# Where and how a two-layer transformer kernel makes its 24 modulation chunks, and the layout of one small projection

## The chip, the cores and the metric

The kernel runs on one core of a Trainium2 chip. The metric is device time in microseconds (us) of one execution. Its engines are TensorE (PE, with its weight loads PEld), VectorE (DVE), ScalarE (ACT), GpSimd (POOL) and SyncE (SP); matmul results go to PSUM, eight banks of 128 partitions by 512 float32. Everything is float32, and a profiled float32 matmul shows as two instructions (x2).

## The reference

Two layers over 256 context and 512 latent tokens of width 1024. What matters here:

```python
for layer in range(DEPTH):
    mod_l = split(silu(c)     @ ada_w[layer] + ada_b[layer], 6)     # 1024 x 6144 weights, 24 MB a layer
    mod_c = split(silu(c_ctx) @ ada_w[layer] + ada_b[layer], 6)
    p = modulate(rmsnorm(x, norm_mix_g), mod[0], mod[1]) @ w_in      # 1024 x 3104, 32 columns are kr
    y = concat(mla(p), swa(p), na(p), retention(p)) * mix_beta
    x = x + mod[2] * (y @ w_out)
    h2 = modulate(rmsnorm(x, norm_ffn_g), mod[3], mod[4])
    x = x + mod[5] * peer_ffn(h2)                                    # product-key experts, gathered rows
return rmsnorm(x_latent, final_norm_g)
```

`mla`, `swa` and `na` are softmax attentions with four heads each; `kr` is a 32-wide key part shared by the heads of `mla`. In the second layer only latent tokens are queries.

## The kernel before, in words

**Tokens.** 768 tokens are six tiles of 128. `hT` holds the normalised input turned, eight blocks of 128 features by 768 tokens; `yT` the mixers' output in the same form. Layer one works on six tiles, layer two on the four latent ones (keys of all six).

**Weights.** SP streams all large weights through `wring`, three slots of 1 MB, in one order fixed by `send`. A slot is sent again once PE signals that it has read it. One modulation chunk (512 of the 6144 columns) takes two slots; twelve chunks make one layer's modulation.

**A modulation chunk.** On PE L486 multiplies the two conditioning vectors by four row blocks of a slot in four 32-column strips of the array at once, for two slots: 16 instructions in the profile. ACT copies the bank out (L885), PE adds the four strips with L474 and the bias with L476 (two matmuls, four instructions), ACT copies the two rows out (L876) and stores them to HBM (L878). Chunks alternate between banks 6 and 7. The first four chunks of layer one's modulation (M=0) come first of all. The other eight stand between the six tiles of the first normalisation (`MOD_BETWEEN`): DVE normalises a tile (L1253, L1254), PE turns it (L510), ACT copies it to `hT` (L926). The twelve chunks of layer two's modulation (M=1) are made in layer one as well: 0 and 1 after the projection c5 and before the state matmuls L716; 2 to 4 behind L716; 5 and 6 between the two halves of the output projection; 7 to 11 between the tiles of the second normalisation (`MOD_BEFORE_FFN`).

**The kr projection.** After the first normalisation L523 makes `kr`: for each of six tiles eight matmuls with a 128x128 block of `hT` as weights and 32 moving columns, 48 in all. ACT copies it to `krrow` (L939). Then the projection chunks follow (L456 for those in token rows, L667 to L679 for those in feature rows).

**Attention.** Each of the three attentions goes over 24 items in layer one (six tiles by four heads; the first eight, of the context, have 256 keys, the others 768, 512 to 640, or 512) and 16 in layer two. PE in iteration i: `scores(i)` (L606, banks 0 to 3), `turn(i-2)`, which turns the probabilities (L618, banks 4 and 5), and for even i `values(i/2-2)` (L647), which makes the output of a pair of items, in bank 6 or 7 by the pair's parity. `scores(i)` waits for the exponential of item i-2, `turn(i)` for its normalisation. ACT in iteration i: exponential of item i (L1014), normalisation of item i-1 (L1021), and for even i from 6 on `y_out(i/2-3)`, which copies a pair's output to `yT` (L1003). DVE: the row maximum (L1325), a reciprocal, and the copy of the turned probabilities (L1344).

**Retention and the rest.** L716 makes six tiles of state updates; DVE chains them to states (L1384), and PE waits for the last (`st`) before the retention loop (L740, L751, L754, L730). Then the output projection (L456 with `yT`) in two chunks, with DVE's gated residual (L1431, L1433) under it, the second normalisation, the first queries of the expert FFN (L790), and the expert stage, which gathers 1280 rows of 8 KB for each of 128 partitions over both layers (L1673).

## Time and profile before

| | us |
|---|---|
| three runs | 4973.15, 4973.56, 4980.19 (median 4973.56) |
| the profiled execution: its own time | 4968.76 |
| its span in the trace | 4967.0 |
| first normalisation, from 59.85 to the start of kr at 116.51 | 56.7 |
| the three attentions of layer one: from 260.0, 337.4 and 508.0 | 77.4, 81.1, 74.7 |
| end of c5 to the retention loop, 667.66 to 707.46 | 39.8 |
| retention loop to the first queries of the FFN, 707.46 to 891.17 | 183.7 |
| expert stage of layer one, about 907 to 2957 | 2050 |

Of the span PE is busy 66%, DVE 63%, POOL 30%, ACT 18%. In the page's slices the 16 DMA engines are at 9 tenths in the expert stages (about 910 to 2950 and 3620 to the end) and at 0 to 3 tenths in the mixer stages, but for the first slice. The page is to be read by stage: in the mixer stages one engine follows another and nothing else is in flight, so that a stretch on PE there moves the end by its whole length; in the expert stages the gathers fix the pace. The times in the rows are us from the start of the span; idle time before a group stands in brackets with what ended it. A window row gives the stretch and its length, then the busy time with the number of instructions of PE, PEld, DVE, ACT and POOL, then the granted TensorE clock (as a share of 2.4 GHz; 1.00 or 0.50 at any one moment, so that a mean lies between), the DMA engines' busy share, and GB/s.

### The profile page before, as it was taken

The page shows a single profiled execution, that of the slowest core. Times are in us where ns is not written, and L with a number is a line of the kernel's source. Part 1 is how long each engine was busy: PE and PEld are TensorE (multiplying, and loading weights), DVE is VectorE, ACT ScalarE, POOL GpSimd, SP SyncE. Part 2 cuts the span into 40 slices and gives each one's busy share as a digit, 9 for nine tenths or more (in the row PEclk, how much of TensorE's full clock was granted, in tenths as well). Part 3 has the DMA queues.
Part 4 walks back from the last instruction along what each step waited for, and adds up shares of the span by engine and source line. Part 5 has one row for each costly group of instructions (what it writes and reads, how often), then busy time and mean ns, then how long its engine had stood idle before and what let it go on. Part 6 is the DMA issues. An engine that isn't in the chain of part 4 may idle for free.

```text
span 4967.0 us, 49025 instructions
## 1 busy us (share of the span) xinstructions
PE 3289.4 (66%) x16328; PEld 1296.2 (26%) x16328; DVE 3127.8 (63%) x8329; ACT 916.4 (18%) x2477; POOL 1492.6 (30%) x1376
## 2 busy tenths in 40 slices
PE   6989898665786555555555558898877455554554
PEld 1455553331232111111111115555422111111111
DVE  1052332587877878778877861513378787877876
ACT  2152321111111111111111121422111111111211
POOL 0000000233444443444444430000043444444443
PEclk8879889887898777777776768788888877777777
DMA  8100033899999999999999971011299999999998
GB/s 285 36 9 26 22 111 122 336 412 416 406 418 415 401 417 406 412 419 405 418 415 406 415 295 45 1 34 39 75 402 395 414 406 418 404 419 416 400 420 345
DMA packets 290751, 1496.73 MB, mean 301 GB/s; under 512 B 25433, under 2 KB 83929, under 8 KB 126657
## 3 DMA queue, kind: packets, MB, share of 16 engines
q0 software_dynamic: 185888, 1347.13, 65.9%
q1 hardware_dynamic: 73680, 114.85, 6.8%
q10 hardware_dynamic: 30928, 31.61, 1.9%
q8 instruction: 129, 2.11, 0.2%
q14 instruction: 126, 1.02, 0.1%
HBM read 1482.91 MB, written 10.58 MB: 301 GB/s over the span
## 4 chain that ended last, share of the span: by engine, by line
DVE 38%; PE 30%; DMA 19%; issue 7%; ACT 4%; POOL 1%; DVEq 1%; ACTq 0%; POOLq 0%; SPq 0%
DMA X<-in_uv_dram,X 17%; DVE X L1552 16%; PE ps L456 9%; PE ps L823 5%; PE ps L606 2%; DVE X L1563 2%; PE ps L647 2%; PE ps L790 2%; ACT X L1170 2%; PE ps L618 1%; POOL X L1673 1%; DVE X L1471 1%; DVE X L1469 1%; DVE X L1472 1%; DVE X L1559 1%
## 5 line engine op out<-in xcount | busy, mean ns | idle before, releaser
L823 PE MATMUL ps<-X 64*64 64x512 f32 x2560 | 1648.7, 778 | 1399.3 <-DVE X L1563 1384.7
L1673 POOL DMA_INDIRECT X<-in_uv_dram,X x1280 | 1417.2, 1107 | 2194.8 <-PE ps L826 1613.4
L1552 DVE CUSTOM_DVE_ANT_0 X<-yT,X 128x1024 f32<-128x1024 f32 x1280 | 1532.4, 1223 | 338.8 <-DMA X<-in_uv_dram,X 290.0
L826 PE MATMUL ps<-X 64*64 64x512 f32 x2560 | 1649.0, 778 | 0.0
L825 PE MATMUL ps<-X 64*64 64x512 f32 x2560 | 1649.0, 778 | 0.0
L824 PE MATMUL ps<-X 64*64 64x512 f32 x2560 | 1648.8, 778 | 0.0
L823 PEld LDWEIGHTS ps<-X 64*64 64x64 f32 x2560 | 360.5, 163 | 2621.0 <-DVE X L1563 1951.9
L1170 ACT ACTIVATE X<-X 128x1 f32<-128x1 f32 x1280 | 258.6, 203 | 2335.7 <-DVE X L1552 2268.9
L825 PEld LDWEIGHTS ps<-X 64*64 64x64 f32 x2560 | 360.7, 163 | 0.0
L826 PEld LDWEIGHTS ps<-X 64*64 64x64 f32 x2560 | 360.6, 163 | 0.0
L824 PEld LDWEIGHTS ps<-X 64*64 64x64 f32 x2560 | 360.5, 163 | 0.0
L790 PE MATMUL ps<-hT,wring 128*128 128x512 f32 (+1 forms) x768 | 314.0, 548 | 2.2 <-ACT hT L926 2.2
L456 PE MATMUL ps<-wring,hT 128*128 128x512 f32 (+2 forms) x736 | 304.8, 576 | 2.0 <-DVE X L1296 1.0
L1563 DVE TENSOR_TENSOR X<-wukv,X 128x128 f32<-128x128 f32 x640 | 187.2, 292 | 68.4 <-DVE X L1559 3.7
L1646 POOL TENSOR_TENSOR X<-X 128x256 f32<-128x256 f32 x32 | 23.0, 722 | 634.9 <-DVE att L1329 625.1
L1559 DVE TENSOR_TENSOR X<-X 128x2 f32<-128x2 f32 x640 | 102.9, 161 | 174.0 <-ACT X L1170 161.9
L606 PE MATMUL ps<-X 64*128 64x256 f32 (+3 forms) x464 | 182.4, 533 | 9.8 <-ACT X L1014 6.6
L1325 DVE TENSOR_REDUCE att<-ps 128x1 f32<-128x512 f32 (+3 forms) x120 | 87.0, 725 | 154.4 <-PE ps L606 152.2
L790 PEld LDWEIGHTS ps<-hT,wring 128*128 128x128 f32 x768 | 141.9, 198 | 161.9 <-issue 153.4
L456 PEld LDWEIGHTS ps<-wring,hT 128*128 128x128 f32 x736 | 138.6, 193 | 163.2 <-issue 159.1
L456 PE MATMUL ps<-wring,yT 128*128 128x512 f32 x320 | 146.6, 620 | 8.2 <-DVE X L1409 3.5
L618 PE MATMUL ps<-ident,X 128*128 128x128 f32 x512 | 103.7, 339 | 51.9 <-ACT X L1021 51.9
(232 smaller groups left out, 3481.5 us busy)
## 6 DMA issues: line engine op xcount, KB each, us to landing
wring<-in_ada_w_dram SPq DMA_DIRECT2D x48, 1024.0 KB
wring<-in_w_in_dram SPq DMA_DIRECT2D x24, 1024.0 KB
wring<-in_peer_wq_dram SPq DMA_DIRECT2D x24, 1024.0 KB
X<-in_uv_dram,X POOLq DMA_INDIRECT x1280
wring<-in_w_out_dram SPq DMA_DIRECT2D x8, 1024.0 KB
X<-scores ACTq DMA_DIRECT2D x64, 128.0 KB
X<-mods ACTq DMA_DIRECT2D x15, 512.0 KB, 6.7
yT<-mods ACTq DMA_DIRECT2D x8, 512.0 KB
```

What stands on the lines that cost most here:

```text
L456: m = pe.matmul(ps[:, t, c0:CH], hT_or_y[0][:, k, t * P:(t + 1) * P], wring[:, g % WRING, kk, c0:CH], start=(k == 0), stop=(k == KD - 1))
L606: m = pe.matmul(ps[:, 2 * (i % 2) + at // 512, at % 512:at % 512 + c], q, k[:, first + done:first + done + c], start=True, stop=True)
L618: m = pe.transpose(ps[:, 4 + b // 4, (b % 4) * P:(b % 4 + 1) * P], pr3[:, i % 3, b * P:(b + 1) * P], ident[:, :])
L790: m = pe.matmul(ps[:, 4 + j % 2, 0:N], by_columns(wq[0])[:, k, j % 2 * P:(j % 2 + 1) * P], hT[:, k, c0:c0 + N], start=(k == 0), stop=(k == ...
L823: pe.matmul(ps[0:HD, h, :], dg(slice(0, HD), s), v0[0:HD], **ends)
L824: pe.matmul(ps[HD:P, 2 + h, :], dg(slice(HD, P), s), v0[HD:P], **ends)
L825: pe.matmul(ps[HD:P, h, :], dg(slice(0, HD), s + 1), v1[0:HD], **ends)
L826: m = pe.matmul(ps[0:HD, 2 + h, :], dg(slice(HD, P), s + 1), v1[HD:P], **ends)
L1170: nc.scalar.activation(agel[:, s:s + 1], adot[:, s:s + 1], ACT.Gelu).then_inc(S("gel"), 1)
L1552: v.tensor_tensor_reduce(uvr[:, slot, 0:D], h2[:, t, :], uvr[:, slot, 0:D], 1.0, 0.0, ALU.mult, ALU.add, adot[:, s_:s_ + 1]).then_inc(S("d ...
L1563: v.tensor_tensor(dgs[:, s_ % DGRING:s_ % DGRING + BATCH, :], ident2.unsqueeze(1).to_broadcast([P, BATCH, HD]), adot[:, both].unsqueeze(2) ...
L1673: g.indirect_dma_start(uvr[:, slot, :], None, a["uv"], bass.IndirectOffsetOnAxis(ap=istages[i % 2][:, s:s + 1], axis=0)).then_inc(S(f"uv{s ...
```

## The change

Four parts.

1. `MOD_LATE` lists 20 chunks: 4 to 11 of M=0 and 0 to 11 of M=1. Six are made in each of the three attentions of layer one (at pairs 0, 2, 4, 6, 8, 10 of 12), the last two in the retention. `late_parts` (the L486 work) stands behind `values(p)`, `late_sum` (the L474 and L476 work) behind `values(p+1)`. The first normalisation, the output projection and the second normalisation have no chunk left in them. SP's order follows.
2. In all attentions of both layers `values` uses bank 7 for each pair and waits for the copy of the pair before it (formerly the one before that); the late chunks have bank 6. ACT's `y_out(p)` moves one iteration up, to i = 2p+5.
3. On ACT `late_rows` and `late_out` (the work of L885, L876, L878 and the bias load) stand behind `y_out`.
4. `kr` is made columnwise in both layers: `wkr` is the weights, 32 columns wide, and `hT` moves, in eight matmuls of 512 and eight of 256 tokens. ACT copies 32x768 out, six small transposes in the middle of the first projection chunk turn it to token rows, and ACT copies those to `krrow`.

```diff
-MOD_BEFORE_FFN = ((7, 8), (9,), (10,), (11,), (), ())
-MOD_EARLY = (2, 5, 7)
-MOD_BETWEEN = ((4, 5, 6), (7,), (8,), (9,), (10,), (11,))
+MOD_LATE = [(0, c) for c in range(MOD_FIRST, ADA_CHUNKS)] + [(1, c) for c in range(ADA_CHUNKS)]
+MOD_PAIRS = (0, 2, 4, 6, 8, 10)
+MOD_KINDS = {"mla": MOD_LATE[0:6], "swa": MOD_LATE[6:12], "na": MOD_LATE[12:18]}
+MOD_LAST = MOD_LATE[18:]
...
+        mod_late = (view(96 * K, [CH]), view(98 * K, [CH]))
...
-            for c in range(1, ADA_CHUNKS):
+            for c in range(1, MOD_FIRST):
                 send(0, a["ada_w"][0], c * CH, "mpp", c + 1, True)
...
-                    after = {len(stream) - 1: mod[:MOD_EARLY[1]], len(stream): mod[MOD_EARLY[1]:MOD_EARLY[2]], len(stream) + 1: mod[MOD_EARLY[2]:]}
+                    after = {1: mod[0:12], 3: mod[12:18], 5: mod[18:]}
...
+                def late_parts(M, c):
+                    pe.wait_ge(S("mrow"), B("mrow", M) + c)
+                    for half in range(2):
+                        g = take(1)
+                        for j in range(GROUP_K):
+                            m = pe.matmul(ps[32 * j:32 * j + 32, 6, :], cT[:, half * GROUP_K + j, :], wring[:, g % WRING, j, :],
+                                          start=(half == 0), stop=(half == 1))
+                        m.then_inc(S("mpp" if half else "w_half"), 1)
+                def late_sum(M, c):
+                    pe.wait_ge(S("mpc"), B("mpc", M) + c + 1)
+                    pe.matmul(ps[0:2, 6, :], pick, mod_late[0], start=True, stop=False)
+                    pe.wait_ge(S(f"ab{c % 2}"), B(f"ab{c % 2}", M) + 16 * (c // 2 + 1))
+                    pe.matmul(ps[0:2, 6, :], ones[0:1, 0:2], mod_late[1][0:1, :], start=False, stop=True).then_inc(S("mps"), 1)
...
-                for t in range(TILES):
-                    for k in range(KD):
-                        m = pe.matmul(ps[:, 7, t * 32:(t + 1) * 32], hT[:, k, t * P:(t + 1) * P], wkr[:, k, :],
-                                      start=(k == 0), stop=(k == KD - 1))
+                for k in range(KD):
+                    pe.matmul(ps[0:32, 6, :], wkr[:, k, :], hT[:, k, 0:CH], start=(k == 0), stop=(k == KD - 1))
+                for k in range(KD):
+                    m = pe.matmul(ps[0:32, 7, 0:TOK - CH], wkr[:, k, :], hT[:, k, CH:TOK], start=(k == 0), stop=(k == KD - 1))
                 m.then_inc(S("kr"), 1)
-                rows_chunk(L, range(TILES), S("c0"), ctx_from=384)
+                def turn_kr():
+                    pe.wait_ge(S("krx"), B("krx", L) + 1)
+                    for t in range(TILES):
+                        m = pe.transpose(ps[:, 7, TOK - CH + t * 32:TOK - CH + (t + 1) * 32], kr_cols[:, t * P:(t + 1) * P], ident[0:32, 0:32])
+                    m.then_inc(S("krp"), 1)
+                rows_chunk(L, range(TILES), S("c0"), turn_kr, ctx_from=384)
...
                     def values(p):
                         pe.wait_ge(S("a_pt"), ab + 2 * p + 2)
-                        if p >= 2:
-                            pe.wait_ge(S("a_ye"), ab // 2 + p - 1)
+                        if p >= 1:
+                            pe.wait_ge(S("a_ye"), ab // 2 + p)
...
+                        p = i // 2 - 2
                         if i >= 4 and i % 2 == 0:
-                            values(i // 2 - 2)
+                            values(p)
+                            if L < LAST and p in MOD_PAIRS:
+                                late_parts(*MOD_KINDS[kind][MOD_PAIRS.index(p)])
+                            if L < LAST and p - 1 in MOD_PAIRS:
+                                late_sum(*MOD_KINDS[kind][MOD_PAIRS.index(p - 1)])
                     pe.wait_ge(S("a_ye"), ab // 2 + N // 2)
+                    if L < LAST:
+                        M, c = MOD_KINDS[kind][-1]
+                        pe.wait_ge(S("mrow"), B("mrow", M) + c + 1)
...
-                    modulation(L + 1, range(0, MOD_EARLY[0]))
+                    late_parts(*MOD_LAST[0])
                 for t in range(TILES):
+                    if L < LAST and t == CT:
+                        late_sum(*MOD_LAST[0])
...
-                    modulation(L + 1, range(MOD_EARLY[0], MOD_EARLY[1]))
-                    pe.wait_ge(S("mrow"), B("mrow", L + 1) + MOD_EARLY[1])
+                    late_parts(*MOD_LAST[1])
+                    late_sum(*MOD_LAST[1])
+                    pe.wait_ge(S("mrow"), B("mrow", L + 1) + ADA_CHUNKS)
...
-                if L < LAST:
-                    modulation(L + 1, range(MOD_EARLY[1], MOD_EARLY[2]))
...
+                def late_rows(M, c):
+                    act.wait_ge(S("mpp"), B("mpp", M) + c + 1)
+                    if (M, c) != MOD_LATE[0]:
+                        M_, c_ = MOD_LATE[MOD_LATE.index((M, c)) - 1]
+                        act.wait_ge(S(f"ms{c_ % 2}"), B(f"ms{c_ % 2}", M_) + 16 * (c_ // 2 + 1))
+                    nc.scalar.activation(mod_late[0], ps[:, 6, :], ACT.Copy).then_inc(S("mpc"), 1)
+                def late_out(M, c):
+                    act.wait_ge(S("mps"), B("mps", M) + c + 1)
+                    if (M, c) != MOD_LATE[-1]:
+                        load_bias(*MOD_LATE[MOD_LATE.index((M, c)) + 1])
+                    nc.scalar.activation(mod_late[0][0:2, :], ps[0:2, 6, :], ACT.Copy).then_inc(S("mrow"), 1)
+                    act.wait_ge(S("mrow"), B("mrow", M) + c + 1)
+                    act.dma_start(mods[M, :, c * CH:(c + 1) * CH], mod_late[0][0:2, :]).then_inc(S(f"ms{c % 2}"), 16)
...
-                        if i >= 6 and i % 2 == 0:
-                            y_out(i // 2 - 3)
+                        p = (i - 5) // 2
+                        if i >= 5 and i % 2:
+                            y_out(p)
+                        if L < LAST and i >= 5 and i % 2 and p in MOD_PAIRS:
+                            late_rows(*MOD_KINDS[kind][MOD_PAIRS.index(p)])
+                        if L < LAST and i >= 7 and i % 2 and p - 1 in MOD_PAIRS:
+                            late_out(*MOD_KINDS[kind][MOD_PAIRS.index(p - 1)])
```

The lines of the changed kernel have other numbers: L488 and L501 are the L486 of before, L476/L478 and L507/L509 its L474/L476, L525 its L510, L627 its L606, L639 its L618, L668 its L647, L458 its L456, L1060 its L1014, L1067 its L1021, L1049 its L1003.

PE, the end of the first normalisation of layer one, kr and the first projection chunk, before:

```order
L486 MATMUL ps<-wring,cT 32x512 x8
L474 MATMUL ps<-X,ones 2x512
L476 MATMUL ps<-X,ones 2x512
L510 MATMUL ps<-ident,X 128x128 x8
L523 MATMUL ps<-wkr,hT 128x32 x48
L456 MATMUL ps<-wring,hT 128x512 x48
L535 MATMUL ps<-ident,X 96x128 x24
```

The same place now; L536 and L538 are the new kr, L544 its transposes:

```order
L525 MATMUL ps<-ident,X 128x128 x48
L536 MATMUL ps<-hT,wkr 32x512 x8
L538 MATMUL ps<-hT,wkr 32x256 x8
L458 MATMUL ps<-wring,hT 128x512 x24
L544 MATMUL ps<-ident,X 128x32 x6
L458 MATMUL ps<-wring,hT 128x512 x24
L556 MATMUL ps<-ident,X 96x128 x24
```

The six turned tiles (48 transposes) stand together, 48 narrow matmuls have become 16 wide ones, and six transposes split the chunk.

PE in the first attention (`mla`) of layer one, the end of the context items, before:

```order
L647 MATMUL ps<-X 64x128 x4
L606 MATMUL ps<-X 128x256
L618 MATMUL ps<-ident,X 128x128 x2
L606 MATMUL ps<-X 128x512
L606 MATMUL ps<-X 128x256
L618 MATMUL ps<-ident,X 128x128 x2
L647 MATMUL ps<-X 64x128 x4
```

The same place now:

```order
L668 MATMUL ps<-X 64x128 x4
L507 MATMUL ps<-X,ones 2x512
L509 MATMUL ps<-X,ones 2x512
L627 MATMUL ps<-X 128x256
L639 MATMUL ps<-ident,X 128x128 x2
L627 MATMUL ps<-X 128x512
L627 MATMUL ps<-X 128x256
L639 MATMUL ps<-ident,X 128x128 x2
L668 MATMUL ps<-X 64x128 x4
L501 MATMUL ps<-wring,cT 32x512 x8
L627 MATMUL ps<-X 128x512
```

Between the values of a pair (L668) and the next scores (L627) stands now either the sum of a chunk (L507, L509) or the parts of one (L501 x8).

ACT at the third pair of the same attention, before:

```order
L1014 ACTIVATE X,att<-ps,att 128x256 [waits a_t,a_nm]
L1021 ACTIVATE X<-X,att 128x256 [waits a_r]
L1003 ACTIVATE yT<-ps,beta 128x128 [waits a_o]
L1014 ACTIVATE X,att<-ps,att 128x256 [waits a_t,a_nm]
L1021 ACTIVATE X<-X,att 128x256 [waits a_r]
L1014 ACTIVATE X,att<-ps,att 128x768 [waits a_t,a_nm]
```

Now:

```order
L1060 ACTIVATE X,att<-ps,att 128x256 [waits a_t,a_nm]
L1067 ACTIVATE X<-X,att 128x256 [waits a_r]
L1049 ACTIVATE yT<-ps,beta 128x128 [waits a_o]
L896 DMA X<-in_ada_b_dram 1x512 [waits mps]
L931 ACTIVATE X<-ps 2x512
L933 DMA mods<-X 2x512 [waits mrow]
L1060 ACTIVATE X,att<-ps,att 128x768 [waits a_t,a_nm]
```

The copy of a pair's output (L1003, now L1049) is followed by a chunk's row copy and its two DMAs, or elsewhere by its 128x512 copy.

## Rows read from the trace of the kernel before

**Rows 1.** Windows: the three attentions of layer one, then a part of `swa`.
```profile
260.00:337.40 77.40, 64.12 (x416) 42.65 (x416) 41.12 (x96) 41.33 (x86) 0.00 (x0) 0.88 0.00 1
337.40:418.50 81.10, 68.62 (x360) 46.40 (x360) 46.87 (x144) 39.20 (x109) 0.00 (x0) 0.73 0.00 1
508.00:582.70 74.70, 64.49 (x320) 40.91 (x320) 39.61 (x114) 33.19 (x85) 10.24 (x15) 0.70 0.00 1
...
340.80:381.20 40.40, 39.52 (x145) 24.75 (x145) 22.14 (x75) 18.79 (x56) 0.00 (x0) 0.50 0.00 1
```

**Rows 2.** Timeline of PE, first normalisation and kr (start, us, instructions).
```profile
34.93 3.64 PE L486 MATMUL ps<-wring,cT 128*32 128x512 f32 x16 [0.95 <-ACT X L876]
...
86.16 1.92 PE L486 MATMUL ps<-wring,cT 128*32 128x512 f32 x16
88.81 1.02 PE L474 MATMUL ps<-X,ones 128*2 128x512 f32 x2 [0.72 <-ACT X L885]
...
90.70 1.09 PE L510 MATMUL ps<-ident,X 128*128 128x128 f32 x8
...
116.51 18.50 PE L523 MATMUL ps<-wkr,hT 128*128 128x32 f32 x96 [1.16 <-issue]
134.82 43.70 PE L456 MATMUL ps<-wring,hT 128*128 128x512 f32 x96
```

**Rows 3.** Timeline of DVE, first normalisation of layer one.
```profile
76.82 2.36 DVE L1240 SCALAR_TENSOR_TENSOR yT<-yT 128x1024 f32<-128x1024 f32 x2 [62.71 <-DMA yT<-in_norm_mix_g_dram]
```

**Rows 4.** Timeline of layer two: normalisation, kr, keys; DVE's and PE's.
```profile
2960.03 1.28 DVE L1253 SCALAR_TENSOR_TENSOR X<-xs,stat,yT 128x1024 f32<-128x1024 f32 x1
...
2975.89 1.97 PE L510 MATMUL ps<-ident,X 128*128 128x128 f32 x8 [0.68 <-DVE X L1254]
2979.02 20.66 PE L523 MATMUL ps<-wkr,hT 128*128 128x32 f32 x96 [1.16 <-issue]
...
3046.42 1.97 PE L552 MATMUL ps<-X,wukv 128*64 128x512 f32 x2 [0.90 <-ACT X L961]
...
3051.27 1.02 PE L552 MATMUL ps<-X,wukv 128*64 128x512 f32 x2
```

**Rows 5.** Timeline of PE in `mla`, one pair of latent items.
```profile
290.50 1.56 PE L606 MATMUL ps<-X 96*128 96x512 f32 x4
...
295.14 0.87 PE L618 MATMUL ps<-ident,X 128*128 128x128 f32 x6 [1.13 <-ACT X L1021]
...
297.41 1.56 PE L606 MATMUL ps<-X 96*128 96x512 f32 x4
```

**Rows 6.** Timeline of PE in `swa`, three starts of a pair.
```profile
372.05 2.50 PE L606 MATMUL ps<-X 64*128 64x256 f32 x6
...
381.36 1.50 PE L606 MATMUL ps<-X 64*128 64x256 f32 x6
...
388.46 1.35 PE L606 MATMUL ps<-X 64*128 64x256 f32 x6
```

**Rows 7.** Timeline of PE from the end of c5 to the retention loop.
```profile
667.66 1.92 PE L486 MATMUL ps<-wring,cT 128*32 128x512 f32 x16
...
681.82 7.25 PE L716 MATMUL ps<-X 128*128 128x128 f32 x48
...
707.46 1.16 PE L740 MATMUL ps<-X 64*128 64x128 f32 x16 [0.95 <-ACT X L876]
```

**Rows 8.** Timeline of DVE, the state chain behind L716.
```profile
689.11 10.66 DVE L1384 SCALAR_TENSOR_TENSOR X<-X,rsm,ps 64x64 f32<-64x64 f32 x36 [4.13 <-PE ps L716]
```

**Rows 9.** Timeline of PE, output projection to the FFN's first queries.
```profile
795.02 1.92 PE L486 MATMUL ps<-wring,cT 128*32 128x512 f32 x16
...
812.28 42.90 PE L456 MATMUL ps<-wring,yT 128*128 128x512 f32 x96
...
891.17 7.17 PE L790 MATMUL ps<-hT,wring 128*128 128x256 f32 x32 [1.11 <-ACT hT L926]
```

**Rows 10.** Timeline of DVE, last tile of the second normalisation.
```profile
873.79 1.22 DVE L1254 TENSOR_TENSOR yT<-yT,X 128x1024 f32<-128x1024 f32 x1
```

More of the change, by code:

```diff
@@ L914, in _, with norm @@
                     load_bias(0, 1)
-                    modulation(0, range(2), ADA_CHUNKS)
+                    modulation(0, range(2), MOD_FIRST)
                     act.wait_ge(S("in"), 16 * 7)
                     squares(0, range(TILES))
-                    modulation(0, range(2, MOD_FIRST), ADA_CHUNKS)
-                def norm(tag, tiles, between=None):
+                    modulation(0, range(2, MOD_FIRST), MOD_FIRST)
+                def norm(tag, tiles):
                     for i, t in enumerate(tiles):
-                        if between:
-                            between(i)
                         act.wait_ge(S("n_ht"), nb_(tag, L) + i + 1)
@@ L1003, in y_out @@
                         nc.scalar.activation(dst, src, ACT.Copy, scale=beta[:, kb:kb + 1]).then_inc(S("a_ye"), 1)
-                    for i in range(N + 6):
+                    for i in range(N + 4):
                         if i < N:
@@ L1082, in _ @@
                     nc.scalar.activation(gate[:, t, :], ps[:, t, :], ACT.Silu).then_inc(S("c5e"), 1)
-                if L < LAST:
-                    modulation(L + 1, range(0, MOD_EARLY[1]), ADA_CHUNKS)
+                for M, c in MOD_LAST if L < LAST else ():
+                    late_rows(M, c)
+                    late_out(M, c)
                 for j in range(len(tiles) + 4):
@@ L1103, in _ @@
                 load_tables(L, 1, ADA_CHUNKS)
[L1104 to L1105 removed]
                 squares(1, tiles)
[L1107 removed]
+                norm(1, tiles)
                 first, rest = groups(L)
```

43 lines of the change are left out of this document (19 added, 24 removed).

## The prediction, written before the changed kernel was run

> **What bounds the kernel now.** I read the page's slices and stage table first: outside the mixer stages the gathers keep the 16 DMA engines busy, and the change touches nothing there, so the expert stages only shift. Then I read the mixer stages as windows: in the three attentions of layer one PE is busy 83 to 86% of the time, and the DMA engines do nothing [rows 1]. Then the timelines, stretch by stretch, each time asking what PE waits for next. The change takes modulation work from places where PE stood in line for weights, copies and tables, and puts it where PE is the busiest engine. What it is worth is the difference of two sums of about 75 us each, so both have to be made with care.
>
> The granted clock enters each term. It was 0.88, 0.73 and 0.70 in the three attentions, and 0.50 over 40.4 us of `swa` in which PE was busy for 39.5 [rows 1]. The same L486 work of a chunk takes 3.64 us at half clock and 1.92 at full [rows 2].
>
> **Price of a chunk on PE.** Parts 1.92 us, sum 1.89 (from the start of L474 to that of the L510 behind it, 88.81 to 90.70) [rows 2]: 3.8 us at full clock, and about 7.4 at half (3.64, and twice 1.89).
>
> **Attention: what is added.** Would PE's idle time cover it? A pair of `mla` items lasts 6.91 us (290.50 to 297.41) with one wait of 1.13 us, that of L618 for ACT's L1021 [rows 5]. The chain behind this wait is: the scores of item j+1, its maximum on DVE, its exponential on ACT, only then the normalisation of item j, which L618 needs. The new parts and sums stand behind `values`, right before the scores of j+1. They push these scores and with them the whole chain, so the wait stays 1.13 us and the chunk is added in full. At half clock PE is busy throughout and nothing could hide either. So 18 chunks x 3.8 = 68.4 us, if all ran at full clock.
>
> Smaller parts of this term. Refill of the array after each insertion: L606 takes 1.56 us behind other work and 1.46 behind scores in the same stage; I take 2 us in all. At the end of each attention PE now waits for a sum and a copy of two rows on ACT instead of one copy: 0.5 us x 3 = 1.5. Sum so far 72. ACT has room: its busy time is 41.3 of 77.4 us [rows 1], and the 1.3 us per chunk of copies and issues come behind the normalisation that PE waits for. The weights have room too: DMA is at 0.00 there [rows 1], and a chunk needs 2 MB per two pairs; in the first normalisation 2 MB came in under 6 us. The single bank costs nothing: the copy of the pair before is issued right after the normalisation for which `turn` waits, and ends while `turn` runs (0.36 us against 0.44 to 0.87 of L618). In layer two the same holds, so I cost this edit at 0; if the copy came late each of 8 pairs would lose at most its 0.4 us, 3 attentions, 10 us.
>
> The clock. Before, half clock took 2 x (1 - 0.88), 2 x (1 - 0.73) and 2 x (1 - 0.70) of the three stages: 18.6 + 43.8 + 44.8 = 107 us. A pair in `swa` took 9.31 us at half clock and 7.10 next to it at full (372.05, 381.36, 388.46) [rows 6], so full clock is worth 24% of such time, 26 us in all. Parts of a chunk are dense: 128 rows in four strips at once, unlike scores with 64 rows. In the L552 rows the clock rose 4 to 5 us into matmuls of 128 rows, which took 1.97 us at 3046.42 and 1.02 at 3051.27 [rows 4]. So I expect the first parts of each attention at half clock and the clock to rise within a few us and then mostly to stay. I take 4 of 18 chunks at half price (4 x 3.6 = +14), two thirds of the 26 us won back in the old work (-18), and +2 because each attention now ends on narrow work and the projection behind it starts at half clock. The attentions of layer one: 72 + 14 - 18 + 2 = **+70 us**. Bounds: all chunks and all old work at full clock, 72 - 26 = 46; the clock by the same shares as before, mean half share 0.46, 72 + 18 x 3.6 x 0.46 = 102.
>
> **First normalisation.** Without chunks it can run as in layer two, where kr starts 18.99 us after the first L1253 (2960.03 to 2979.02) [rows 4]. In layer one the tables were ready at 76.82 and the scaling took 2.36 [rows 3]: 76.8 + 2.6 + 19.0 = 98.4 instead of 116.51 [rows 2], 18.1 us. The tables' DMAs, issued from 62.1 on, shared the queue with chunk weights that no longer move then (the queue moved some 5 MB to 76.8, half of it tables). They may land 0 to 6 us sooner; I take 4. Together **-22 us**.
>
> **kr.** It was 18.3 us in layer one (116.51 to 134.82) and 20.66 in layer two, all but the start at half clock [rows 2, 4]. Now 8 wide and 8 half-wide matmuls are worth 12 of 512 columns: at 0.89 us 10.7 at full clock, 21 at half. Before it stand only transposes, at half clock in layer two (1.97 us for eight) [rows 4], so it begins at half. If it raises the clock after 4.6 us, as dense work does, it takes 4.6 + 16.4 / 2 = 12.8, and the projection behind it starts at full clock (43.70 us [rows 2] would be 41.8). Less 0.7 us for six transposes: -5.5 - 1.9 + 0.7 = -6.7 in layer one, -7.9 - 1.9 + 0.7 = -9.1 in layer two. Together **-16 us**. Its 32 columns fill a quarter of the array, and no row shows what that does to the clock: at half throughout it is +1 us with the transposes and about 3 in both layers.
>
> [...]
>
> **Retention.** Five chunks stood between 667.66 and the loop at 707.46 [rows 7], two remain. New order: parts 1.92, L716 7.25 with a sum of 1.9 inside it, so L716 ends at 678.7. What is late next is DVE's state chain, 10.66 us behind the last L716 [rows 8]: the loop starts at 689.6. The second chunk (3.8 us on PE, its weights fetched as before by 675.7) and ACT's copies fit under the chain. PE idles before the loop, so L740 runs at half clock, 0.9. **-17 us**.
>
> **Output projection.** Its second half waited from 795.02 to 812.28 for two chunks [rows 9]; DVE had freed the banks by then. 17.3, and 1.2 because L456 no longer starts at half clock (42.90 for 96, against 41.6). **-18.5 us**.
>
> **Second normalisation.** DVE's last tile ends at 873.79 + 1.22 = 875.0 [rows 10]. From the start of the last tile's transposes to the next matmul there are 3.13 us in layer two (2975.89 to 2979.02) [rows 4], so L790 starts at 878.2 instead of 891.17 [rows 9]: 13.0, less 2.2 since PE has idled and L790 starts at half clock. **-11 us**.
>
> **Sum.** -22 - 16 - 17 - 18.5 - 11 = -84; +70; net **-14 us**. The profiled execution's own time was 4968.8 (span 4967.0), which gives 4955; the median of the runs shown lies 4.8 above it, so I predict **4959**.
>
> **Rivals.** (1) The clock does not rise in the attentions, and each insertion pays by the old shares: +102 against -84, +18, 4991: slower. For it: 40.4 us of `swa` at 0.50 although PE was busy. Against it: chunk parts are denser than anything there. It decides from a mean price of 5.2 us a chunk on. Chance 0.20. (2) The dense parts hold the clock up throughout: 46 - 84 = -38, 4935. For it: the first normalisation held full clock with the same matmuls, transposes and waits from 86 to 115. Against: context items and the ends of the stages are thin. 0.20. (3) kr stays at half clock: 19 us less gain, net +5, 4978, no change. For it L523 and the quarter of the array; against it L552, which fills half. 0.20. (4) PE's waits swallow part of the chunks, say 1.1 us at each of 36 insertions, 40 us: net -54, 4920. The chain above speaks against it. 0.05. My forecast has 0.35. That the work isn't moved as said I exclude: the order shows it.
>
> **Numbers.** About 0.2% (10 us) is what the runs shown can tell from no change (their spread was 7 us). Faster: two thirds of the forecast's 0.35 (0.23), all of (2) and (4) (0.25), a little of (3): 0.50. Slower: nearly all of (1), a third of (3): 0.24. Same: 0.26. Range 4935 to 4992: from (2) to (1), with the unknown landing of the tables (4 us either way) inside; (4) and the worst of (1) are left out. The forecast's own range is 4948 to 4971.
>
> **What would show it.** Right: kr starts near 94 in layer one and takes about 13 us in both; the wait of L639 (was L618) stays at 1.1 us in `mla`; L501 mostly at 1.92; the three attentions 70 us longer together, with mean clocks above 0.9, 0.8, 0.8; the retention loop released by the state chain; the projection's halves back to back. Wrong: L501 at 3.64 in most pairs; L536 at half clock to its end; attentions longer by over 85; or a wait of PE for `wring`, a row copy or the pair's copy that I cost at nothing.

## The result, and the profile after

Measured: 4946.40 us (median of 5 runs, 4945.98 to 4951.99), against 4973.56 before; the ratio is 0.9947, 95% interval 0.9936 to 0.9958. That is 27 us faster by the medians and 26 by the ratio, inside the range 4935 to 4992, and 13 us below the predicted 4959. In a second group of runs (E9 below) the changed kernel came to 0.9949 (0.9935 to 0.9962). The profiled execution took 4945.98 us (span 4944.2), 22.8 less than that of before, which is the difference that the stages below add up to.

The windows of the three attentions of layer one, with the columns of [rows 1] (first is `mla`, then `swa`, then `na`):

```profile
226.17:324.51 98.34, 83.48 (x536) 43.09 (x537) 41.02 (x96) 46.81 (x97) 0.00 (x0) 0.94 0.37 129
324.51:436.06 111.55, 95.98 (x480) 48.01 (x481) 46.64 (x144) 44.93 (x120) 0.00 (x0) 0.76 0.33 109
525.61:616.12 90.51, 75.24 (x440) 36.51 (x441) 39.63 (x114) 38.67 (x96) 11.26 (x16) 0.91 0.40 137
```

From the first scores of each stage to the first instruction of the next they took 77.36, 81.06 and 74.62 us before. They are now 21.0, 30.5 and 15.9 us longer, 67.4 together. Six chunks went into each. The granted clock, 0.88, 0.73 and 0.70 in [rows 1], is higher in all three, by most in `na`. The DMA share is now 0.33 to 0.40 where it was nothing, and no instruction of PE waits for `wring` there.

PE's timeline from the first normalisation to the queries' transposes, then the key part in layer two, answering to [rows 2, 4]:

```profile
87.20 1.97 PE L525 MATMUL ps<-ident,X 128*128 128x128 f32 x8 [0.68 <-DVE X L1301]
90.33 9.19 PE L536 MATMUL ps<-hT,wkr 128*32 128x512 f32 x16 [1.16 <-issue]
99.36 3.62 PE L538 MATMUL ps<-hT,wkr 128*32 128x256 f32 x16
102.90 20.87 PE L458 MATMUL ps<-wring,hT 128*128 128x512 f32 x48
123.70 0.56 PE L544 MATMUL ps<-ident,X 32*128 32x32 f32 x6
124.18 20.87 PE L458 MATMUL ps<-wring,hT 128*128 128x512 f32 x48
144.89 1.04 PE L556 MATMUL ps<-ident,X 128*96 128x128 f32 x8
...
2963.66 1.97 PE L525 MATMUL ps<-ident,X 128*128 128x128 f32 x8 [0.69 <-DVE X L1301]
2966.78 9.68 PE L536 MATMUL ps<-hT,wkr 128*32 128x512 f32 x16 [1.16 <-issue]
2976.30 3.62 PE L538 MATMUL ps<-hT,wkr 128*32 128x256 f32 x16
```

The key part starts at 90.33 (116.51 before) and takes 12.6 and 13.1 us (18.3 and 20.5 before). L538 runs at full clock: 16 records of 256 columns in 3.62 us, half of what L536's 16 of 512 columns would take at that rate. L536 at 9.19 lies between the 7.2 of full clock and twice that, so the clock rose inside it. It stood at half before: the transposes ahead of it take 1.97 us for eight, against 1.09 for eight at full clock in [rows 2]. DVE's tables (answering to [rows 3]) came 8 us sooner:

```profile
68.74 2.36 DVE L1287 SCALAR_TENSOR_TENSOR yT<-yT 128x1024 f32<-128x1024 f32 x2 [54.33 <-DMA yT<-in_norm_mix_g_dram]
```

One pair of `mla` with a chunk's parts in it (answering to [rows 5]), and two of the starts in `swa` ([rows 6]):

```profile
263.56 1.92 PE L501 MATMUL ps<-wring,cT 128*32 128x512 f32 x16
265.42 1.56 PE L627 MATMUL ps<-X 96*128 96x512 f32 x4
266.81 0.82 PE L639 MATMUL ps<-ident,X 128*128 128x128 f32 x6
267.47 1.46 PE L627 MATMUL ps<-X 96*128 96x512 f32 x4
270.06 0.87 PE L639 MATMUL ps<-ident,X 128*128 128x128 f32 x6 [1.14 <-ACT X L1067]
270.87 1.53 PE L668 MATMUL ps<-X 128*64 128x128 f32 x24
272.33 1.02 PE L507 MATMUL ps<-X,ones 128*2 128x512 f32 x2
273.28 1.02 PE L509 MATMUL ps<-X,ones 1*2 1x512 f32 x2
...
333.29 3.64 PE L501 MATMUL ps<-wring,cT 128*32 128x512 f32 x16
...
340.55 1.86 PE L507 MATMUL ps<-X,ones 128*2 128x512 f32 x2
342.34 1.86 PE L509 MATMUL ps<-X,ones 1*2 1x512 f32 x2
```

In `mla` the wait for ACT's normalisation is 1.14 us, as before (1.13), so the chunk is added in full and PE waits nowhere else. The sum's rows have two records for each matmul; L509 moves as many columns as L507, from one row instead of 128. In `swa` parts and sums ran at half clock or partly so.

From the end of c5 to the retention loop, and around the output projection ([rows 7 to 10]); first PE, then DVE's state chain:

```profile
702.71 1.92 PE L501 MATMUL ps<-wring,cT 128*32 128x512 f32 x16
...
712.21 1.92 PE L501 MATMUL ps<-wring,cT 128*32 128x512 f32 x16
714.85 1.02 PE L507 MATMUL ps<-X,ones 128*2 128x512 f32 x2 [0.72 <-ACT X L925]
715.80 1.01 PE L509 MATMUL ps<-X,ones 1*2 1x512 f32 x2
723.07 2.08 PE L772 MATMUL ps<-X 64*128 64x128 f32 x16 [6.26 <-issue]
...
790.78 62.07 PE L458 MATMUL ps<-wring,yT 128*128 128x512 f32 x144 [0.71 <-ACT yT L1147]
859.57 1.94 PE L525 MATMUL ps<-ident,yT 128*128 128x128 f32 x8 [6.72 <-DVE yT L1301]
...
875.82 9.10 PE L819 MATMUL ps<-hT,wring 128*128 128x256 f32 x32 [1.11 <-ACT hT L968]
```

```profile
712.32 10.65 DVE L1431 SCALAR_TENSOR_TENSOR X<-X,rsm,ps 64x64 f32<-64x64 f32 x36 [5.30 <-PE ps L747]
```

The state chain ends at 722.97 and the loop starts at 723.07: the wait of 6.26 us, which the view puts down to "issue", is that for DVE. The halves of the projection stand in one row of 144 records.

### The profile page after: what moved, and what is told of

Its sections match the earlier page's. It is cut to its first block, busy times and chain, and to the rows that moved or that the text cites. A ratio compares the mean times of both kernels' runs of the same rounds, so it can differ in the third digit from the quotient of the medians.

```text
span 4944.2 us, 48806 instructions
## 1 busy us (share of the span) xinstructions
PE 3247.7 (66%) x16212; PEld 1259.8 (25%) x16212; DVE 3128.9 (63%) x8329; ACT 913.5 (18%) x2479; POOL 1495.9 (30%) x1376
## 3 DMA queue, kind: packets, MB, share of 16 engines
q14 instruction: 125, 1.02, 0.1%
## 4 chain that ended last, share of the span: by engine, by line
DVE 39%; PE 30%; DMA 19%; issue 7%; ACT 4%; POOL 1%; DVEq 0%; ACTq 0%; POOLq 0%; SPq 0%
DMA X<-in_uv_dram,X 18%; DVE X L1599 16%; PE ps L458 9%; PE ps L852 5%; DVE X L1610 2%; PE ps L627 2%; PE ps L819 2%; PE ps L668 2%; ACT X L1217 2%; DVE X L1516 1%; DVE X L1518 1%; DVE X L1519 1%; DVE X L1606 1%; PE ps L639 1%; PE ps L706 1%
## 5 line engine op out<-in xcount | busy, mean ns | idle before, releaser
L819 PE MATMUL ps<-hT,wring 128*128 128x512 f32 (+1 forms) x768 | 317.9, 553 | 2.2 <-ACT hT L968 2.2
L458 PE MATMUL ps<-wring,hT 128*128 128x512 f32 (+2 forms) x736 | 303.0, 573 | 2.5 <-DVE X L1343 1.0
L1610 DVE TENSOR_TENSOR X<-wukv,X 128x128 f32<-128x128 f32 x640 | 187.4, 293 | 68.4 <-DVE X L1606 2.8
L819 PEld LDWEIGHTS ps<-hT,wring 128*128 128x128 f32 x768 | 144.1, 201 | 163.7 <-issue 153.8
L458 PEld LDWEIGHTS ps<-wring,hT 128*128 128x128 f32 x736 | 137.1, 191 | 163.2 <-issue 159.8
L627 PE MATMUL ps<-X 64*128 64x256 f32 (+3 forms) x464 | 166.4, 492 | 10.4 <-ACT X L1060 6.7
L458 PE MATMUL ps<-wring,yT 128*128 128x512 f32 x320 | 145.0, 616 | 8.2 <-DVE X L1456 3.5
L639 PE MATMUL ps<-ident,X 128*128 128x128 f32 x512 | 96.0, 320 | 60.2 <-ACT X L1067 60.2
```

The source lines that it names most:

```text
L458: m = pe.matmul(ps[:, t, c0:CH], hT_or_y[0][:, k, t * P:(t + 1) * P], wring[:, g % WRING, kk, c0:CH], start=(k == 0), stop=(k == KD - 1))
L627: m = pe.matmul(ps[:, 2 * (i % 2) + at // 512, at % 512:at % 512 + c], q, k[:, first + done:first + done + c], start=True, stop=True)
L819: m = pe.matmul(ps[:, 4 + j % 2, 0:N], by_columns(wq[0])[:, k, j % 2 * P:(j % 2 + 1) * P], hT[:, k, c0:c0 + N], start=(k == 0), stop=(k == ...
L1610: v.tensor_tensor(dgs[:, s_ % DGRING:s_ % DGRING + BATCH, :], ident2.unsqueeze(1).to_broadcast([P, BATCH, HD]), adot[:, both].unsqueeze(2) ...
```

## The experiments

The stages are compared by one measure throughout, the time from PE's first instruction of a stage to its first of the next, in us, from the profiled execution of each kernel. In this table c2 to c3 stands between `swa` and `na`, and "loop" is the retention loop up to the output projection. E7 and E8 have one execution each, the others 4 to 12 runs. The kernel before came to 4973.56, 4972.26, 4981.17 and 4978.75 in the four groups of runs, so totals of different groups are compared by their ratio to the kernel before of the same group: an expected total stands against 4973.56 times the measured ratio.

```
kernel                     kr1    mla    swa     na   loop | kr2   na2
before                   61.85  77.36  81.06  74.62  41.25 | 53.39 60.83
E1 key part alone        54.10  77.04  80.87  77.76  41.49 | 44.38 57.46
E2 one bank alone        63.47  77.32  81.05  74.61  41.24 | 53.77 60.88
changed                  54.56  98.34 111.55  90.51  41.99 | 44.90 57.48
E9 changed again         55.39 101.44 108.62  91.76  41.99 | 44.33 57.47
E7 one matmul more       55.34  97.97 114.96  96.91  42.00 | 45.01 60.85
E8 two matmuls more      55.19 100.71 107.23  91.77  41.99 | 44.92 57.49
E3 parts twice           54.42 110.10 117.60 101.54  41.99 | 44.78 57.47
E4 sums twice            54.69 110.96 113.69 112.28  41.75 | 44.14 54.10
E5 swa's six to loop     55.18  98.50  83.70  94.81  55.98 | 45.08 60.86
E10 the same again       54.52  98.30  83.58  90.85  52.11 | 44.39 57.47
E6 na's six to loop      54.61  98.36 104.74  76.77  55.97 | 44.81 57.31
E11 bias in row 98       54.62  94.22  96.50  88.93  42.00 | 45.00 60.83
E12 E5 and E11           54.74  94.29  80.91  88.01  47.09 | 45.08 60.84
```

(kr1 and kr2: key part and first projection of layers one and two; na2: `na` of layer two.)

**E1, the key part alone.** The kernel before with this edit, and what the change has around it:

```diff
-for t in range(TILES):
-    for k in range(KD):
-        m = pe.matmul(ps[:, 7, t * 32:(t + 1) * 32], hT[:, k, t * P:(t + 1) * P], wkr[:, k, :], ...)
+for k in range(KD):
+    pe.matmul(ps[0:32, 6, :], wkr[:, k, :], hT[:, k, 0:CH], ...)
+for k in range(KD):
+    m = pe.matmul(ps[0:32, 7, 0:TOK - CH], wkr[:, k, :], hT[:, k, CH:TOK], ...)
```

> The kernel before with only the key part made columnwise (8 + 8 matmuls of 32 rows out, then six small transposes) in both layers; modulation, banks and everything else as before. My theory: the key part's gain is its own and owes nothing to the moved chunks. In the changed kernel the stretch from its first matmul to the first transpose of the queries went from 61.85 to 54.56 us in layer one and from 53.39 to 44.90 in layer two, -7.3 and -8.5; so here -16 us, 4957 to 4958. The first matmuls (L536's counterpart) run at half clock in layer two (9.7 us) and, since dense chunk sums stand close before them in layer one, mostly at full there (7 us), which could make layer one's gain up to 2 us larger. Rival: the gain needs the idle PE before it in the changed kernel, or the eviction and the turn show as a wait here: then -8 to -10 us, 4964.

Measured: 4954.69 against 4972.26, ratio 0.9965 (0.9952 to 0.9978), 17 us faster by the ratio; by stages 7.8 in layer one and 9.0 in layer two. The gain is the key part's own. One detail was wrong: in layer one the 16 records of 512 columns did not run at full clock throughout, although chunk sums stood close before them.

```profile
115.67 8.72 PE L522 MATMUL ps<-hT,wkr 128*32 128x512 f32 x16 [1.16 <-issue]
124.23 3.62 PE L524 MATMUL ps<-hT,wkr 128*32 128x256 f32 x16
```

They took 8.7 us where full clock takes 7.2. Here too `na` of layer two is 57.46 us instead of 60.83, with no edit near it, and `na` of layer one 3.1 longer.

**E2, one bank alone.**

```diff
-if p >= 2: pe.wait_ge(S("a_ye"), ab // 2 + p - 1)
+if p >= 1: pe.wait_ge(S("a_ye"), ab // 2 + p)
...
-ps[HD * e:HD * e + HD, 6 + p % 2, 0:P]
+ps[HD * e:HD * e + HD, 7, 0:P]
...
-for i in range(N + 6): ...  if i >= 6 and i % 2 == 0: y_out(i // 2 - 3)
+for i in range(N + 4): ...  if i >= 5 and i % 2: y_out((i - 5) // 2)
```

> The kernel before with only the attention output in one bank (7), values waiting for the pair before to be copied, and the copy issued one item earlier. Layer two's last attention was 3.4 us shorter in the changed kernel (65.39 to 62.04 us) although no work was moved there. My theory: that is where the clock's falls happened to lie, not the bank; so here each attention is as long as before within 1 us unless its start shifts, and the time is 4971 to 4976. Rival: the earlier copy or the single bank shortens na by itself, 3 us in each layer: 4966 to 4969. Second rival: values now wait for the copy, up to 0.4 us at 8 pairs of each attention: 4980.

Measured: 4974.18, ratio 1.0009 (0.9996 to 1.0023). Each attention is within 0.1 us of before, `na` of layer two at 60.88. In these stages the bank costs and gives nothing, and both rivals (3 us gained in each `na`, 0.4 us lost at each pair) fall.

**E3 and E4, parts or sums twice.** In the changed kernel, in the attentions of layer one only:

```diff
 for half in range(2):
     g = take(1)
+    for r in range(2):   # E3
     for j in range(GROUP_K): m = pe.matmul(ps[32 * j:32 * j + 32, 6, :], cT[...], wring[...], ...)
...
+for r in range(2):       # E4
     pe.matmul(ps[0:2, 6, :], pick, mod_late[0], start=True, stop=False)
     m = pe.matmul(ps[0:2, 6, :], ones[0:1, 0:2], mod_late[1][0:1, :], start=False, stop=True)
```

> The changed kernel with each chunk's parts in the three attentions multiplied twice into the same sums (the modulation values are then too large, their amounts of work in the rest the same): 18 x 1.92 = 34.6 us more dense work on PE at full clock. My theory: dense work in the attentions raises the granted clock of what stands round it, most where it makes up more of the time; mla is nearly all at full clock (0.94) and pays 11.5 us, na 0.91 pays 8 to 11, swa, at 0.76, rises and pays only 4 to 10; together +24 to +32, 4970 to 4978. Rival: the clock keeps the shares it has (0.94, 0.76, 0.91) and the price is 12.2 + 14.3 + 12.5 = 39 us, 4985.

> The changed kernel with the two matmuls of each chunk's sum issued twice in the three attentions (the second start overwrites the first, the values stay): 18 x 1.89 = 34.0 us more at full clock, the same columns as the parts but 128 rows into 2 columns, and one row into 2. My theory: these columns hold the clock less than the parts do, since half of them stream a single row; so mla and na pay full price, 11.3 each and up to 2 more, and swa 12 to 17: together +35 to +42, 4981 to 4988, more than the doubled parts cost for the same time on PE. Rival: every busy us counts alike, and the price is that of the doubled parts within 3 us.

Measured: 4979.93, ratio to before 1.0017 (1.0007 to 1.0028), and 4991.59, 1.0041 (1.0027 to 1.0055). E3's modulation values are too large, so everything behind works on other numbers. By the ratios the price over the changed kernel is 35 us for E3, and 47 for E4, with an interval of 8 to 9 us either way: both above what I expected (24 to 32, 35 to 42), though the intervals reach into these ranges; E3's rival (the clock keeps its shares, 39) isn't excluded by them. The profiled executions are the fastest of their groups, +26.5 and +33.7 us against the changed kernel's. From the first scores of `mla` to the retention loop E3 adds 27.2 us in them for 34.6 us of matmuls and E4 40.7 for 34.0, and these two sums are inside what I expected. E4's rival, the same price within 3 us, falls by the stages (13.5 us apart) and narrowly by the ratios (12, plus or minus 9). The split of E4 was not as expected: `swa` paid 2.1 us and `na` 21.8. The windows of `swa` and `na` in E4:

```profile
337.77:451.46 113.69, 97.43 (x505) 47.22 (x505) 46.83 (x144) 45.01 (x120) 0.00 (x0) 0.85 0.33 112
543.95:656.23 112.28, 100.12 (x464) 42.14 (x465) 39.53 (x114) 38.65 (x96) 11.27 (x16) 0.78 0.34 117
```

More of the same work lifted the clock of `swa` (0.76 to 0.85) and sank that of `na` (0.91 to 0.78). So one execution of one kernel does not tell what a microsecond of such work does to the clock, and the doubled sums don't show by themselves what a single row does.

**E7 and E8, the start shifted.** In the changed kernel, as `between` of the second projection of layer one, once or twice:

```diff
+pe.matmul(ps[0:2, 6, :], pick, hT[:, r, 0:CH], start=True, stop=True)
```

> The changed kernel with one more matmul (128 rows into 2, 512 columns, result unused) in the middle of layer one's second projection: all of the mixer behind it starts 0.9 to 1.0 us later, and nothing else is changed. It asks how much of a stage's length hangs on the instant at which it starts. My theory: na of layer two was 60.8 or 57.5 us long in kernels that do the same work there, so a shift alone moves a stage's length by some 3 us: mla within 1, swa and na each within 5 us of 111.55 and 90.51, layer two as in the changed kernel unless its own start moves against the clock. Rival: all stages as in the changed kernel within 0.5 us, and the differences between kernels come from their instructions.

> The same with two such matmuls, a shift of 1.8 to 2.0 us. My theory as for one; if the price of swa's six chunks (30.5 us, against 15.9 in na) is luck of the start, one of the two shifts brings swa below 106 us or na above 95; if it belongs to the stages, swa stays at 108 to 114 and na at 88 to 94 in both.

Measured: 4960.74 and 4959.58 (one run each; `mla` started at 230.77 and 231.79, 4.6 and 5.6 us later than in the changed kernel: 1.5 and 2.3 us come between key part and `mla`, where the shift stands, 2.3 and 2.7 from the start of the key part, behind the tables' landing, and the rest from the key part's stage). `swa` was 114.96 and 107.23 us, `na` 96.91 and 91.77: 7.7 and 5.1 us apart, with the same instructions. The two `swa`:

```profile
328.74:443.70 114.96, 100.43 (x481) 51.60 (x481) 46.86 (x144) 44.90 (x120) 0.00 (x0) 0.72 0.32 106
```

```profile
332.50:439.73 107.23, 89.91 (x481) 45.55 (x481) 46.68 (x144) 44.94 (x120) 0.00 (x0) 0.81 0.34 114
```

PE's busy time moved by 10.5 us with the clock, DVE's and ACT's by 0.2. E7 met the mark that I had set for luck (`na` over 95), and the one for the stage (`swa` 108 to 114 in both) was missed on either side. A stage with the same instructions differs by up to 10 us between executions that reach it at different moments (`swa` 104.74 to 114.96 over five kernels in which it is the same). The shift isn't shown to be the cause: E5 and E10 are one kernel, and their `na` took 94.81 and 90.85 us, and no kernel was profiled twice with the same start. So 15.9 and 30.5 us as single values are in part luck; the means over kernels that do the same there still differ: six chunks cost 21.9 us in `mla` (99.1, seven kernels, less 77.2, three), 27.6 in `swa` (109.4, five, less 81.9, six) and 16.8 in `na` (92.8, six, less 75.9, four).

**E5, E10 and E6, six chunks in the retention loop.** `MOD_KINDS` of one stage is empty and `MOD_LAST` has eight chunks instead of two. ACT's work follows, and its copy of a tile's turned outputs moves to the head of an iteration. In the loop over tiles:

```diff
 m.then_inc(S("inner"), 1)
+if L < LAST and 2 + i < len(MOD_LAST): late_parts(*MOD_LAST[2 + i])
...
 m.then_inc(S("ro"), 1)
+if L < LAST and 2 + i < len(MOD_LAST): late_sum(*MOD_LAST[2 + i])
...
-ps[:, 6 + j % 2, b * P:(b + 1) * P]   # turn_out, and ACT's copy
+ps[:, 7, b * P:(b + 1) * P]
```

> The changed kernel with the six chunks of swa moved into the retention loop of layer one (one for each of its six tiles, parts behind L772, sum behind the tile's outputs, bank 6; the outputs' transposes use bank 7 alone in both layers). My theory: swa was the dearest place (+30.5 us for six chunks, 81.06 to 111.55) and gives all of it back; in the loop, 42 us at half clock before, the dense parts raise the clock, a head that takes 1.28 us at half takes 0.67 at full, and six chunks of 3.8 us come on top of some 24 to 28 us of old work: the loop takes 47 to 55 us, +5 to +13, and the sum is -18 to -25: 4922 to 4930. Rival: the loop stays at half clock with chunks of 7.3 us: +44 - 30.5 = +14, 4960. Second rival: the clock rises, but the chain of DVE and ACT (product, mean, squares, copy) keeps each tile at 7 us or more and the chunks come in full on top: +23 - 30.5 = -8, 4938.

> As the kernel with swa's chunks in the loop, but na's six are moved there and swa keeps its own. My theory: na's six cost only 15.9 us where they stood (74.62 to 90.51, since they raised na's clock from 0.70 to 0.91), so the same move gives 15 us less than swa's: the loop +5 to +13, net -3 to -11, 4936 to 4944. Rival: what a stage costs with six chunks is luck of where the clock's falls lie, and both moves give the same within 4 us.

> The kernel with swa's six chunks in the retention loop again, beside the changed kernel. By stages it should be 111.55 (104 to 115) less 81 to 84 in swa, and plus 14.0 in the loop: 7 to 20 us below the changed kernel, 14 likeliest.

Measured: E5 4936.17, ratio 0.9904 (0.9888 to 0.9921); E10 4929.67, 0.9907 (0.9892 to 0.9922), 24 us below the changed kernel of the same group (E9, 4953.81); E6 4944.40, 0.9927 (0.9911 to 0.9942). The loop took 55.98, 52.11 and 55.97 us instead of 41.99: six chunks for 10 to 14 us, though at full clock they are 22.8 us of PE. The changed kernel's loop, its first tile in part, then E5's loop, its second tile in part and the start of the third:

```profile
727.08 0.74 PE L783 MATMUL ps<-X 128*128 128x128 f32 x2
727.62 0.95 PE L786 MATMUL ps<-X 128*128 128x64 f32 x4
728.36 0.74 PE L783 MATMUL ps<-X 128*128 128x128 f32 x2
```

```profile
712.67 1.23 PE L772 MATMUL ps<-X 64*128 64x128 f32 x8
713.83 3.32 PE L501 MATMUL ps<-wring,cT 128*32 128x512 f32 x16
...
718.47 0.44 PE L785 MATMUL ps<-X 128*128 128x128 f32 x2
718.75 0.56 PE L788 MATMUL ps<-X 128*128 128x64 f32 x4
719.14 0.44 PE L785 MATMUL ps<-X 128*128 128x128 f32 x2
...
721.80 0.71 PE L772 MATMUL ps<-X 64*128 64x128 f32 x8
722.82 1.92 PE L501 MATMUL ps<-wring,cT 128*32 128x512 f32 x16 [0.30 <-ACT X L937]
```

From the end of the second chunk's parts on the loop stands at full clock, and a head (from one L783, now L785, to the next) takes 0.67 us instead of 1.28. In the windows (the changed kernel's loop, then E5's) the clock goes from 0.50 to 0.87:

```profile
723.07:765.06 41.99, 39.63 (x198) 37.35 (x198) 21.41 (x41) 5.82 (x12) 6.00 (x6) 0.50 0.00 0
```

```profile
703.57:759.55 55.98, 50.46 (x318) 24.92 (x318) 21.71 (x41) 13.21 (x26) 6.00 (x6) 0.87 0.65 226
```

The theory holds. E5 and E6 came to totals inside their ranges by the ratios (4926 and 4937); E10's 24 us are more than the 7 to 20 expected, since the loop took 52.11 us. The loop came 1 us above its range in E5 and E6 and inside it in E10. The rival of chunks at half price falls, and with it the second one (waits of DVE and ACT). E6 gave 8 us less than E5 by the medians, between the 15 that I expected and its rival's "within 4": `swa` happened to be at 104.74 in it.

**E9, E11 and E12.** E9 is the changed kernel again, and came as expected in each point. E11 takes the single-row matmul out:

```diff
-mod_late = (view(96 * K, [CH]), view(98 * K, [CH]))
+mod_late = (view(96 * K, [CH]), view(96 * K, [CH])[98:99, :])
...
-pe.matmul(ps[0:2, 6, :], pick, mod_late[0], start=True, stop=False)
-pe.matmul(ps[0:2, 6, :], ones[0:1, 0:2], mod_late[1][0:1, :], start=False, stop=True)
+pe.matmul(ps[0:2, 6, :], pick[0:99, :], mod_late[0][0:99, :], start=True, stop=True)
...
-nc.scalar.activation(mod_late[0], ps[:, 6, :], ACT.Copy)
+nc.scalar.activation(mod_late[0][0:98, :], ps[0:98, 6, :], ACT.Copy)
```

The selection matrix `pick` gets ones in row 98 besides.

> The changed kernel again, unaltered, beside the others of this group. The key part's start in layer one (90.33 us in its first profile, 88.7 to 93.3 in kernels that are alike up to there) and swa and na (111.55 and 90.51) should come again within what the shifted kernels showed: start 88 to 94, swa 104 to 115, na 90 to 97; 0.993 to 0.996 of the kernel before.

> The changed kernel with the bias of a late chunk brought by its DMA into row 98 of the copied parts, and the selection matrix with ones in that row, so that one matmul of 99 rows makes the sum and the matmul of a single row (L509, 1.01 us) goes in all twenty late chunks. My theory: 0.95 us go at each of 20 chunks, and since a single row of 512 columns seemed to do little for the clock (doubled sums cost 40.6 us for 34.0 of work, doubled parts 27.1 for 34.6), its removal costs no clock: attentions of layer one -17 to -21, retention about 0 (its sums stand beside the state chain), -17 to -21 in all, 4925 to 4930 against 4946. Rival: the busy columns count whatever their rows, the clock falls more often without them, and only 8 to 12 us are left of the gain, 4935.

> Both: swa's six chunks in the retention loop, and the bias in row 98. My theory: the two add up, and the loop saves 6 more times 0.95 us while it stays at full clock (50 to 51 us instead of 55.98): -14 and -19 against the changed kernel, 4909 to 4918. Rival: without the single-row matmuls the loop's clock falls back to half for part of it (60 us or more), and the gain over the changed kernel is 20 us or less, 4926.

Measured, all beside a kernel before of 4978.75: E9 4953.81, 0.9949 (0.9935 to 0.9962); E11 4923.81, 0.9893 (0.9877 to 0.9909); E12 4917.36, 0.9881 (0.9865 to 0.9898). E11 is 30 us below E9, more than the 17 to 21 that I expected. Against the means above, `mla` is 4.9 us shorter, `swa` 12.9 and `na` 3.8, 21.6 in all where 17 were 18 matmuls at full clock; the c4 stage is another 1.7 shorter. Of the profiled execution's lead over E9's, 3.7 us lie ahead of the key part, where the two kernels are the same. The clock of the three stages in E11:

```profile
224.60:318.82 94.22, 79.36 (x524) 43.86 (x525) 41.02 (x96) 46.76 (x97) 0.00 (x0) 0.92 0.38 131
318.82:415.32 96.50, 78.33 (x468) 42.82 (x469) 46.84 (x144) 44.90 (x120) 0.00 (x0) 0.86 0.38 128
505.37:594.30 88.93, 75.10 (x428) 38.76 (x429) 39.65 (x114) 38.64 (x96) 11.25 (x16) 0.82 0.39 135
```

In `swa` it is above the 0.72 to 0.82 of the five kernels with L509, in `mla` inside their 0.91 to 0.94 (seven), and in `na` at the lower end of their 0.82 to 0.91 (six). So removing the single row cost no clock on the whole, and the rival with only 8 to 12 us of gain falls. That it raised `swa`'s clock by its nature, and not by its start, isn't shown by one kernel. E12 is the fastest of all: 36 us below E9, 1.2% below before. Its `swa` is at 80.91 and its loop at 47.09 us, clock 0.93; the loop came 3 us below what I expected and `mla` as in E11. Its gain over E11 is 6 us by the medians and 4.2 by the profiled spans, less than the 14 that I had given to the move: `swa` gives back 15.6 us and not 26, since E11 had already made its chunks cheaper, the loop takes 5.1, and the output projection's stage (up to the FFN's first queries) is 5.2 us longer (115.38 against 110.23). There 144 records of L459 took 65.12 us instead of 62.07; the outputs' transposes, which now share one bank, explain little of it, since E5 and E10 have the same order and are only 1.0 and 1.4 us longer than the changed kernel there, with 62.07 for the 144 records. Why the clock was lower in E12 stays open.

## Why the prediction was right

By its own steps, forecast and measured by the profiled execution:

```
step                                   forecast   measured
first normalisation                      -22       -26.2
key part, both layers                    -16       -15.8  (E1: -16.8)
attentions, with c4 behind them          +70       +69.1  (67.4 + 1.7)
retention                                -17       -18.7  (-19.4, and +0.7 in the loop)
output projection                        -18.5     -18.7
second normalisation                     -11       -13.0, and 3.1 lost behind it
na of layer two                            0        -3.4
queries' stretch of layer one, tail        0        -0.5, +1.4
sum                                      -14.5     -22.7
```

**First normalisation.** The step from the tables to the key part was right to the tenth (21.6 us from DVE's scaling to L536, forecast and measured). What was mis-sized is the term for the tables' landing, 4 us of "0 to 6": it was 8.1. Eleven kernels alike up to there started the key part at 88.6 to 93.3 us, 90.9 in the mean; before, E1 and E2, which are alike up to there, started it at 116.51, 115.67 and 114.11. By these means the gain is 24.6 us, and 1.6 of the 26.2 are chance.

**Key part.** Price, cause and place were right, and E1 shows that it stands by itself. The rival in which its 32 columns stay at half clock falls: L538 takes 3.62 us in both layers, full clock, in a quarter of the array's columns.

**Attentions.** The sum was right, and so was the reason why nothing of a chunk is hidden: the wait for ACT stayed at 1.14 us. The rivals with +102, +46 and swallowed chunks fall. The terms were right too: the chunks' instructions were busy for 85.3 us (43.67, 21.40 and 20.18 for L501, L507 and L509), against 71.3 at full clock (18 times 1.92 and twice 1.02), so the surcharge for half clock was 14 us, as forecast. That leaves about -15 for the old work, forecast -14.5 (-18, and 3.5 for the refill and the ends; what I called a refill is the 0.1 us between two durations of L606, and no run shows its cause). But both corrections together are hardly anything: all chunks at full clock, 68.4 us, would have come as close. And that the sum is right to a microsecond is luck: the three stages together are 68.8 us longer than before in E9, which is the same kernel, 76.8 in E7 and 66.7 in E8. The picture of the clock was right in `mla` and `na` only. I forecast parts "mostly at 1.92" and mean clocks above 0.9, 0.8 and 0.8. In `swa` the mean was 0.76, and none of six parts took 1.92 us: their sum was 16.36 us, against 13.10 in `mla` and 14.21 in `na` (11.5 at full clock).

```profile
226.17:324.51 98.34, 13.10 (x96) 2.69 (x96) 0.94 0.37 129
324.51:436.06 111.55, 16.36 (x96) 3.20 (x96) 0.76 0.33 109
525.61:616.12 90.51, 14.21 (x96) 2.92 (x96) 0.91 0.40 137
```

(Windows with L501's instructions alone: length, PE, PEld, clock, DMA share, GB/s.) That `na` paid less than its chunks' 22.8 us and `swa` more had no place in my sum, which took one mean price for the three. Ten of the 14 us of surcharge fell on `swa`. A busy PE alone didn't keep the clock up: in E7's `swa` it was busy for 100.43 of 114.96 us at a clock of 0.72.

**Retention, projection, second normalisation.** What was named as late next was late next each time: the state chain, nothing, and DVE's last tile. The 2.2 us that I took off for a start at half clock are there (L819 9.10 us for 32 records, [rows 9] 7.17); the whole stretch up to layer two is 3.1 us longer.

**`na` of layer two** gave 3.4 us that no step foresaw. E1 has them without any edit near, and E2 with the bank's edit has not; over the fourteen kernels it took 54.1, 57.3 to 57.5 or 60.8 to 60.9 us with the same instructions. It is the clock: 0.66 in the window of before, 0.73 in the changed kernel's, 0.81 in E4's. Nor is the stage a good measure by itself, for in E5, E7 and E12 it took 60.8 us and `swa` of layer two 3.4 us less than elsewhere (63.2 instead of 66.6). The two together took 127.5 us in before, E2 and E11, 120.7 in E4 and 123.9 to 124.1 in the other ten. E11 has all four parts of the change and not the 3.4 us: they are luck, and 13% of the measured gain.

## What to carry to other kernels

Work moved to a busy engine is not paid by its own duration alone but also by what the clock does there: the same six chunks, 22.8 us at full clock, cost 28 us in one attention, 22 and 17 in the others and 10 to 14 in a loop of thin matmuls that had been at half clock throughout. So look for the stretch at half clock whose work is thin, and put dense work there first. Before a few microseconds of a stage's length are read as the effect of an edit, profile the kernel again, or with its start shifted by a microsecond or two, and see what the stage does by itself.

## What the runs showed of the hardware

- A stage's length can change by 3 to 10 us with the same instructions, from one execution to another that reaches it at a different moment: `swa` 104.74 to 114.96 us (clock 0.82 to 0.72), `na` of layer two 57.47 or 60.83 (clock 0.73 or 0.66).
- A sum into two columns takes 0.95 us a matmul whether it moves 128 rows or one; putting the bias into a spare row of the other operand saved at least that time (E11: the three attentions 21.6 us shorter by the means, for 18 matmuls of 0.95).
- A loop of matmuls with 64 to 128 columns each stood at a granted clock of 0.50 with PE busy for 39.63 of 41.99 us; with one chunk a tile among them it had 0.87, 0.96 and 0.87 (E5, E10, E6).
- 32 columns of the array are enough for the clock to rise: the key part reached full clock within 9.7 us of its start in both layers, behind transposes at half clock.
